# Expert blocks of 64 token slots, computed in two 64-column groups of the array

## What is computed

```
gate, eid = top-2 experts of a token inside its best group of 8   # 32 experts, D_EXPERT 512
dest      = place of each (token, expert) pair, experts padded to whole blocks
y         = (silu(x @ w_gate[e]) * (x @ w_up[e])) @ w_down[e]     # for each block of one expert
h         = h + sum over the two experts of gate * y
```

## Time and profile before

| | |
|---|---|
| median of the timed runs | 3724.7 us (3715.61 to 3728.29) |
| the profiled execution | 3695.65 us, its span 3694.0 us, mean granted clock 0.944 |
| TensorE busy | 3157.5 us (85%) |
| VectorE, ScalarE, GpSimd busy | 1523.9, 1120.6, 183.2 us |
| DMA over the span | 463.52 MB, 125 GB/s |
| last 114 us (combining) | no TensorE, DMA share 0.82 |

### The profile page before, as it was taken

How to read it: one execution, slowest core, us unless ns; L and a number is a source line. 1 busy time by engine, 2 the same in 40 slices (tenths; PEclk the granted TensorE clock), 3 DMA queues, 4 the chain that set the end, 5 groups by cost and what they waited for, 6 DMA issues and landing times. The chain is left out here.

```text
span 3694.0 us, 63731 instructions
## 1 busy us (share of the span) xinstructions
PE 3157.5 (85%) x24000; PEld 2104.5 (57%) x24001; DVE 1523.9 (41%) x3383; ACT 1120.6 (30%) x2480; POOL 183.2 (5%) x200
## 2 busy tenths in 40 slices
PE   6999999999688887888887699946999999999970
PEld 5778777777455555877787545523444444444430
DVE  3666666676577775332332277730000000000013
ACT  2334333343477776222222133410111111111110
POOL 0000000000000000000000000021000000000013
PEclk9999999999799998999999899968999999999985
DMA  5121111111301101121222343254855556877648
GB/s 205 52 71 55 60 51 58 65 57 58 101 8 45 44 10 61 54 66 55 66 66 68 121 177 129 103 161 148 318 198 189 191 183 213 316 249 262 208 164 308
DMA packets 214384, 463.52 MB, mean 125 GB/s; under 512 B 20352, under 2 KB 86016, under 8 KB 212608
## 3 DMA queue, kind: packets, MB, share of 16 engines
q1 hardware_dynamic: 185616, 385.06, 29.7%
q0 software_dynamic: 19456, 41.99, 4.1%
q10 hardware_dynamic: 9072, 33.03, 2.4%
HBM read 343.01 MB, written 117.03 MB: 125 GB/s over the span
## 5 line engine op out<-in xcount | busy, mean ns | idle before, releaser
L285 PE MATMUL pj_big<-pj_xnT,pj_w_in 128*128 128x256 f32 x2816 | 636.7, 382 | 10.6 <-issue 9.2
L285 PEld LDWEIGHTS pj_big<-pj_xnT,pj_w_in 128*128 128x128 f32 x2816 | 539.1, 192 | 93.3 <-issue 16.9
L1751 DVE TENSOR_TENSOR ex_hh<-ex_sg,ex_pu 128x128 f32<-128x128 f32 x94 | 35.4, 418 | 949.6 <-PE ex_pu L1690 949.6
L1690 PE MATMUL ex_pg<-ex_wg,ex_xT 128*128 128x512 f32 x752 | 336.2, 600 | 12.8 <-DMA ex_wd<-in_w_exp_down 11.3
L1705 PE MATMUL ex_py<-ex_wd,ex_hT 128*128 128x512 f32 x752 | 331.1, 593 | 0.0
L1690 PE MATMUL ex_pu<-ex_wu,ex_xT 128*128 128x512 f32 x752 | 330.4, 592 | 0.0
L1690 PEld LDWEIGHTS ex_pg<-ex_wg,ex_xT 128*128 128x128 f32 x752 | 143.4, 192 | 199.5 <-issue 199.5
L1690 PEld LDWEIGHTS ex_pu<-ex_wu,ex_xT 128*128 128x128 f32 x752 | 142.9, 190 | 179.9 <-issue 179.9
L1223 PE MATMUL mg_po<-mg_w_out,mg_mix 128*128 128x512 f32 x512 | 226.8, 601 | 4.1 <-DMA mg_w_out<-in_w_out 2.4
L707 ACT ACTIVATE at_e<-at_sc,at_nmx 128x512 f32<-128x512 f32 (+3 forms) x320 | 196.8, 621 | 107.2 <-DVE at_nmx L746 107.1
L1705 PEld LDWEIGHTS ex_py<-ex_wd,ex_hT 128*128 128x128 f32 x752 | 139.0, 190 | 157.4 <-issue 157.4
(11 more groups left out here) (268 smaller groups left out, 4738.1 us busy)
## 6 DMA issues: line engine op xcount, KB each, us to landing
ex_wg<-in_w_exp_gate SPq DMA_DIRECT2D x32, 2048.0 KB, 9.3
ex_wu<-in_w_exp_up SPq DMA_DIRECT2D x32, 2048.0 KB, 14.4
ex_wd<-in_w_exp_down SPq DMA_DIRECT2D x32, 2048.0 KB, 18.6
slots_s<-ex_yb ACTq DMA_DIRECT2D x47, 512.0 KB, 4.8
chunks_s<-pj_st SPq DMA_DIRECT2D x32, 642.0 KB, 3.9
rw_raw<-chunks_s SPq DMA_DIRECT2D x32, 642.0 KB, 4.9
slots_s<-rw_zero SPq DMA_DIRECT2D x32, 512.0 KB, 5.7
pj_xt<-in_x SPq DMA_DIRECT2D x20, 512.0 KB, 3.7
```

The source lines that it names most:

```text
L285: ins = pe.matmul(out, lhs, rhs, start=(k == 0), stop=(k == KC - 1))
L1690: ins = pe.matmul(out[:, :], xT[:, k, :], w[:, k, :], start=(k == 0), stop=(k == KC - 1))
```

## The change

A block now holds 64 slots (`BT`). The list of slots, the places of the experts and the loops count blocks of 64. In the work on a block, the array's 128 columns form two groups of 64, and the same 64 tokens are the loaded operand in either group:

- Gate and up: the output columns of an expert (512) are cut in four quarters; group j = 0 forms quarters 0 and 1, group j = 1 quarters 2 and 3, and `part` says which of the two. For each of eight k, each j has one matmul of 64 output rows and 128 streamed columns. The result of a group lies in its half of the partitions of `pg` and `pu`.
- Down: group n forms output columns 512 n to 512 n + 511, streaming 512 columns.
- The gathered tokens lie as half rows: partitions 0 to 63 hold the first 512 columns of the 64 tokens, 64 to 127 the second. Four transposes then turn the block. GpSimd computes the numbers of half rows (twice the token number plus `c_side`) with one instruction, and loads the token numbers two blocks ahead.
- `hh` is formed and transposed in two parts, one transpose each; the first transpose of hh stands ahead of the transposes of the next tokens, the second behind the first two down matmuls.

```diff
+BT = 64
-NB = 2 * S // P + NE
+NB = 2 * S // BT + NE
...
-            chain(dve.tensor_tensor(more[:, :, :], wide(base[:, :], NT), middle(blocks[:, :], NE), ALU.is_gt))
+            chain(dve.tensor_tensor(more[:, :, :], wide(base[:, :], S // BT), middle(blocks[:, :], NE), ALU.is_gt))
...
         @block.gpsimd
         def _(pool):
+            def load(b):
+                rows = dr["slot_tok"][bass.ds(b * BT, BT), :]
+                pool.dma_start(raw[:, :], rows.unsqueeze(0).broadcast_to([2, BT, 1])).then_inc(s_raw, 16)
+
+            def index(b):
+                pool.wait_ge(s_raw, 16 * b + 16)
+                pool.sem_inc(s_apart, 1)
+                pool.tensor_scalar(idx[:, :], raw[:, :], 2.0, side[:, :], ALU.mult, ALU.add).then_inc(s_idx, 1)
+                pool.wait_ge(s_idx, b + 1)
+                pool.sem_inc(s_apart, 1)
+
             def gather(b):
-                pool.dma_start(idx[:, :], dr["slot_tok"][bass.ds(b * P, P), :]).then_inc(s_idx, 16)
-                pool.wait_ge(s_idx, 16 * b + 16)
-                pool.sem_inc(s_apart, 1)
-                pool.indirect_dma_start(xb[:, :], None, dr["hn"], bass.IndirectOffsetOnAxis(idx[:, 0:1], 0))\
-                    .then_inc(s_x, 16)
+                pool.indirect_dma_start(xb[:, :], None, hn2, bass.IndirectOffsetOnAxis(idx[:, 0:1], 0)).then_inc(s_x, 16)
 
             def body(b, x):
+                pool.wait_ge(s_x, 16 * b + 16)
+                index(b + 1)
+                load(b + 2)
                 pool.wait_ge(s_px, b + 1)
                 pool.sem_inc(s_apart, 1)
                 gather(b + 1)
...
         @block.tensor
         def _(pe):
...
+            def inner(out, w, part):
+                for k in range(KC):
+                    lhs = xT[:, k % 4, k // 4 * BT:(k // 4 + 1) * BT]
+                    for j in range(2):
+                        c0 = 2 * P * j + P * part
+                        ins = pe.matmul(out[j * BT:(j + 1) * BT, 0:P], lhs, w[:, k, c0:c0 + P],
+                                        start=(k == 0), stop=(k == KC - 1))
                 return ins
...
+            def down(part, j, x, start=False, stop=False):
+                for n in range(2):
+                    ins = pe.matmul(py[n * BT:(n + 1) * BT, :], hT[:, part, j * BT:(j + 1) * BT],
+                                    wd[x][:, 2 * j + part, n * HD:(n + 1) * HD], start=start, stop=stop)
+                return ins
 
             def body(b, x):
                 pe.wait_ge(s_xT, b + 1)
-                pe.wait_ge(s_hh, 2 * b + 2)
-                for out, w, done in ((pg, wg[x], s_pg), (pu, wu[x], s_pu)):
-                    for k in range(KC):
-                        ins = pe.matmul(out[:, :], xT[:, k, :], w[:, k, :], start=(k == 0), stop=(k == KC - 1))
-                    ins.then_inc(done, 1)
+                for part in range(2):
+                    pe.wait_ge(s_hh, 2 * b + 1 + part)
+                    inner(pg[part], wg[x], part).then_inc(s_pg, 1)
+                    inner(pu[part], wu[x], part).then_inc(s_pu, 1)
+                pe.wait_ge(s_hh, 2 * b + 3)
+                transpose_h(0)
                 pe.wait_ge(s_x, 16 * b + 32)
-                transpose_x(range(KC - 2))
...
+                transpose_x()
+                pe.wait_ge(s_yb, b + 1)
+                pe.wait_ge(s_hT, 2 * b + 1)
+                down(0, 0, x, start=True)
+                pe.wait_ge(s_hh, 2 * b + 4)
+                transpose_h(1)
+                down(0, 1, x)
                 pe.wait_ge(s_hT, 2 * b + 2)
...
+                down(1, 0, x)
+                down(1, 1, x, stop=True).then_inc(s_py, 1)
...
-                act.activation(sg[:, :], pg[:, :], ACT.Silu).then_inc(s_sg, 1)
-                for part, at in enumerate(PARTS):
+                for part in range(2):
+                    act.wait_ge(s_pg, 2 * b + 1 + part)
+                    act.activation(sg[:, part, :], pg[part][:, 0:P], ACT.Silu).then_inc(s_sg, 1)
+                for part in range(2):
                     act.wait_ge(s_phT, 2 * b + 1 + part)
...
-                act.activation(yb[:, :], py[:, :, :].rearrange("p a n -> p (a n)"), ACT.Copy).then_inc(s_yb, 1)
+                act.activation(yb[:, :], py[:, :], ACT.Copy).then_inc(s_yb, 1)
```

More of the change, by code:

```diff
@@ L1485, in dispatch @@
         ones = m.sb("ones", [P, P])
-        blocks = m.sb("blocks", [P, NT])
+        blocks = m.sb("blocks", [P, S // BT])
         picked = m.sb("picked", [P, NT, NE])
@@ L1490, in dispatch @@
         base = m.sb("base", [P, NE])
-        more = m.sb("more", [P, NE, NT])
+        more = m.sb("more", [P, NE, S // BT])
         nb = m.sb("nb", [P, NE])
@@ L1498, in dispatch @@
         ids = m.sb("ids", [P, NT], I32)
[L1499 removed]
+        zero = m.sb("zero", [P, (NB + 4) * BT // P], I32)
         pr = m.ps("pr", [P, 512])
@@ L1593, in experts @@
         dispatch(nc, io, dr, keep, lambda sp: [weights(sp, bass.ds(x, 1), x) for x in range(2)])
+        HD = D // 2
         ident = m.sb("ident", [P, P])
         cols = m.sb("cols", [P, PC_N])
+        side = m.sb("side", [P, 1])
+        raw = m.sb("raw", [P, 1], I32)
         idx = m.sb("idx", [P, 1], U32)
[L1598 to L1608, removed]
+        xb = m.sb("xb", [P, HD])
+        xT = m.sb("xT", [P, 4, P])
+        sg = m.sb("sg", [P, 2, P])
+        hh = m.sb("hh", [P, 2, P])
+        hT = m.sb("hT", [P, 2, P])
+        yb = m.sb("yb", [P, HD])
+        px = m.ps("px", [P, 4, P])
+        pg = [m.ps(f"pg{n}", [P, 512]) for n in range(2)]
+        pu = [m.ps(f"pu{n}", [P, 512]) for n in range(2)]
+        phT = [m.ps(f"phT{n}", [P, 512]) for n in range(2)]
+        py = m.ps("py", [P, 512])
         s_const = m.sem("const")
         s_done = m.sem("done")
-        s_idx = m.sem("idx_ld")
+        s_raw = m.sem("raw_ld")
+        s_idx = m.sem("idx_done")
         s_x = m.sem("x")
@@ L1668, in body @@
                 gather(b + 1)
+            pool.wait_ge(s_const, 48)
+            load(0)
+            index(0)
+            load(1)
             gather(0)
             turns(pool, body)
+            last = pool.value_load(keep["blocks"][0:1, 1, NE - 1:NE], min_val=0, max_val=NB - 2)
+            n = pool.value_load(keep["blocks"][0:1, 0, NE - 1:NE], min_val=1, max_val=S // BT)
+            pool.wait_ge(s_raw, 16 * last + 16 * n + 32)
+            pool.sem_inc(s_apart, 1)
         @block.tensor
@@ L1674, in _, with transpose_x @@
         def _(pe):
-            def transpose_x(ks):
-                for k in ks:
+            def transpose_x():
+                for k in range(4):
                     ins = pe.transpose(px[:, k, :], xb[:, k * P:(k + 1) * P], ident[:, :])
-                return ins
[L1680 to L1683, removed]
+                ins.then_inc(s_px, 1)
@@ new lines, in inner, with transpose_h @@
+            def inner(out, w, part):
[5 more added lines that the diff above has]
+                                        start=(k == 0), stop=(k == KC - 1))
+                return ins
+            def transpose_h(part):
+                pe.transpose(phT[part][:, 0:P], hh[:, part, :], ident[:, :]).then_inc(s_phT, 1)
```

65 lines of the change are left out of this document (26 added, 39 removed).

## The result

The changed kernel takes **3794.9 us** (median of 4 runs, 3779.4 to 3795.6), the kernel before 3723.2 (3715.6 to 3728.3) on the same chip: a ratio of 1.018 with the interval 1.015 to 1.022. It is slower by about 72 us; 3627 was forecast.

What follows compares the result with a forecast made beforehand. TensorE's streaming was taken to bound the expert stage, transfers a near second. 79 x 12.0 plus 3 waits and 2.9 cold start gave 954 us (-103); with the other terms -98, so 3724.7 - 98 = 3627 us, range 3570 to 3750.

Steps and rivals of the forecast that it cites:

- Number of blocks, 79: Expert stage: by counted tokens, 17 experts have two blocks of 64 and 15 have three, 79 in place of 47.
- Two column groups overlap fully: Gate, up and down: both groups stream side by side, 7.0 us for gate and up, 3.4 for down.
- rivals 1, 2 and 3: Gate, up, down: groups take turns, 4438 us (15%); half overlap by order, 3706 (11%); weight loads on the path, 3912 (4%).
- 12.0 us a block: Expert block of 64: 7.04 gate and up, 3.43 down, 0.65 transposes, 0.72 round trips, 0.17 wait for hT.
- the two round trips: TensorE switching between full-array transposes and tiled work, twice a block: 0.36 us each, 0.72 together.
- the wait for hT: First down matmul waits for the first part of hT after its transpose: 0.17 us a block left uncovered.
- Dispatch +1.1: Dispatch: comparison and sum over blocks go from 512 to 1024 elements, adding 1.1 us.
- Start of the experts +4: Expert start: GpSimd waits for constants, converts and issues one more load before the gather, adding 4 us.
- The write of the result, priced at nothing: End of each block: the yb copy must be through before the next down, 7 us later; taken as hidden.
- Weights, waits of 3 us by a landing of 18.5: Expert stage: TensorE's waits for weights shrink from 11.3 to 3 us, with down weights landing after 18.5.
- The floor that the prediction named: Weight loading: 17 experts cannot go under about 22 us each, however fast the blocks are.
- The turning point: Expert block: the change turns from gain to loss once a block takes over 13.3 us.

Runs made afterwards that it cites:

- split_both: As split_write, with each block's token-number load also split into two loads of 64; 3596.2 us, ratio 0.968 to the kernel before.
- split_write: Changed kernel with each block's result written as two writes of 64 rows in place of one rearranged write; 3625.8 us, ratio 0.976 to the kernel before.
- split_apart: As split_write, but gate and up run all eight k of one column group before the other's; 3946.0 us, ratio 1.062.

## Why the prediction was right and wrong

- **Number of blocks, 79: right.** 79 copies of a result, 5056 records each of gate and up.
- **Two column groups overlap fully: right**, and rivals 1, 2 and 3 are out. In the timeline of the changed kernel 32 records of `pu` last 1.92 us, (1.92 - 0.27)/31 = 0.053 in the mean; one by one, a pair starts every 0.109 us and the two of a pair 6 to 7 ns apart. No weight load shows on the path.
- **12.0 us a block: right within 2%.** An undisturbed block is 11.77 us, 11.82 where the expert changes. In split_both, from gate to gate, with such a change:

```profile
2809.75 1.97 PE L1706 MATMUL ex_pg<-ex_wg,ex_xT 128*64 128x128 f32 x32
2810.00 0.60 ACT L1759 ACTIVATE ex_yb<-ex_py 128x512 f32<-128x512 f32 x1 [2.54 <-PE ex_py L1715]
...
2816.89 0.33 PE L1711 MATMUL ex_phT<-ex_ident,ex_hh 128*128 128x128 f32 x1
...
2817.67 1.08 PE L1715 MATMUL ex_py<-ex_wd,ex_hT 128*64 128x512 f32 x4
...
2821.57 1.92 PE L1706 MATMUL ex_pg<-ex_wg,ex_xT 128*64 128x128 f32 x32
```

  Gate and up take 7.14 us to the first transpose, where 7.04 was taken. The rest is 11.82 - 7.14 = 4.68 for 4.97. Less 3.43 for down and 0.65 for the transposes that leaves 0.60 for the two round trips and the wait for hT, which were set at 0.72 + 0.17; the two are not told apart here.
- **Dispatch +1.1: right** (comparison to last scatter, 47.1 to 48.2). **Start of the experts +4: right within 1** (last scatter to first gate, 16.8 to 20.0). The gather stays hidden.
- **The write of the result, priced at nothing: wrong, and this is the step that failed.** The working said only "The yb copy must be through before the next down, 7 us later: hidden." It looked at the copy and not at what the copy waits for. The rows of split_both give the true limit. A Silu pass must start in time for the transpose at +7.14 us of a block, and from the start of the copy to that transpose it was 2807.49 - 2805.18 = 2.31 us, so the copy can start at +4.83 at the latest. Undisturbed it starts at +0.25 and its write is issued 0.77 later. The next copy's limit is then 11.77 + 4.83 - 1.02 = 15.6 us after the issue. The old write's 4.9 us would fit easily. The new one was a different pattern, which I read in the diff and gave the old one's duration: at 17.3 it is 1.7 us late, and TensorE waited 1.91. Over the stage 23 of the 79 writes land after more than 15.6 us, and the transpose of hh waits 20 times.
- **Weights, waits of 3 us by a landing of 18.5: wrong through the same step.** The landing became 29.0. From the first gate of an expert to the issue of the down weights for the one after the next it is 2813.42 - 2809.75 = 3.67 us in split_both, so an expert of two blocks must last 32.7 us and lasts 23.5. With the write mended they land after 20.1, 23.8 in all, and the waits are 3.7 us. The floor that the prediction named was the right one, with the wrong landing time in it. Together the two waits are 142.3 us where 3 were forecast, and the clock that the records show lowered behind them adds about 35.
- **The sum.** The turning point was set at 13.3 us a block; with 1120.7/79 = 14.2 the changed kernel is beyond it, by waits and not by the array. With the write mended the stage is 961.9 (split_write) or 945.4 us (split_both) where 954 was forecast. So the forecast fits another kernel than the one that was changed: I priced the arithmetic of the edit and not the pattern of one of its transfers. That split_write's 3625.8 us lies on the forecast of 3627 is partly luck: the blocks were 0.2 us shorter than summed and the waits for weights 18.4 us and not 3, and the kernel before ran in 3711.7 us beside it and not in 3724.7. The differences are -86 us for it and -116 for split_both, with -98 forecast.

Blocks at 11.77 us each would take 930 us; beyond that waits, changes of expert and the lower clock add 191 us in the changed kernel and 16 in split_both.

## What to carry to other kernels

Of every transfer that an edit rewrites, read the slowest dimension of its pattern first: here a rearranged write with a 2 in front used two DMA engines, and more of its price fell on the large transfers beside it (74 us) than on the engine that waited for its buffer (50 us). When a block is halved, everything that has one block's time (a single buffer, the write out of it, the next expert's weights) has half, so each needs its own limit in us and its own landing time, with the transfer as it is now and not as it was. Two writes, each over a plain block of rows, did better here than one rearranged write over both.

## What was not expected of the hardware

- Two column groups of 64 on the same 128 rows run side by side in float32: a pair of 128-column records every 0.109 us, where a single group took 0.109 a record. The loads of 137 ns in the mean vanish in these steps, although both groups use all rows. The Trainium skill ("TensorE: Matmul & The Clock Gate", section "The mechanism") says in its list of what overlaps that loads overlap with matmuls in flight only when the row group differs; the measurement decides against it here. Just above, the same section also allows loads into a background weight buffer, and that the trace does not contradict.
- TensorE's records start ahead of older ones of the other column group: in split_apart 14 of each 32 steps are half steps, 7 at each change of the group. So "nothing reorders it", said above of the engines' programs, does not hold for the starts of TensorE's records.
- A narrow write of 256 KB per block, for which nobody waits, moves the landing of 2 MB of weights to 30.6 us, and in the changed kernel TensorE waits while some two of the 16 DMA engines work.
- Open: the 0.6% of a reordered write over all 16 engines, and the 0.8% of split_both over split_write.
